# A first product pair taken before the norm's divisor, modulation products moved, and empty scatter slots skipped, in a two-network transformer kernel

## What is computed

```
mod = silu(c) @ ada_w[i] + ada_b[i]             # 1024 -> 6 * 1024: shift, scale, gate, twice
h = modulate(rms_norm(x, norm_g[i, 0]), sh_a, sc_a)      # x/rms * g * (1 + scale) + shift
y = mixer(h)
x = x + g_a * rms_norm(y, norm_g[i, 1])
h = modulate(rms_norm(x, norm_g[i, 2]), sh_f, sc_f)
y = square(relu(h @ ffn_w1[i])) @ ffn_w2[i]              # 1024 -> 4096 -> 1024
x = x + g_f * rms_norm(y, norm_g[i, 3])
```

```
mod = silu(c) @ w_mod[l] + b_mod[l]                      # and the same for a context vector
a = silu(xb @ w_gate[e]) * (xb @ w_up[e]);  yb = a @ w_down[e]
routed = zeros.at[slot_tok].add(yb * slot_w)
```

## Time and profile before

| what | us |
|---|---|
| runs, median (lowest to highest) | 3743.69 (3739.06 to 3747.0), 3 runs |
| the profiled execution: its own time | 3742.4 |
| its span, first to last instruction | 3740.7 |
| PE busy | 3328.8 (89%) |
| DVE busy | 1403.1 (38%) |
| ACT, POOL busy | 504.6 (13%), 427.4 (11%) |
| HBM read and written | 849.95 MB and 36.18 MB, 237 GB/s over the span |

### The profile page before, as it was taken

One profiled execution on the slowest core, in us unless ns is written; L12 is line 12 of the kernel. 1 busy time (PEld: TensorE's weight loads), 2 busy tenths in 40 slices (PEclk: granted clock), 3 DMA queues, 4 the chain that ended last, 5 costly groups with the idle time before them and its releaser, 6 DMA issues.

```text
span 3740.7 us, 40275 instructions
## 1 busy us (share of the span) xinstructions
PE 3328.8 (89%) x14228; PEld 2231.6 (60%) x14228; DVE 1403.1 (38%) x3085; ACT 504.6 (13%) x1021; POOL 427.4 (11%) x482
## 2 busy tenths in 40 slices
PE   3799897998999998899998988899894998999998
PEld 2678785887887886778664533344442676333333
DVE  7555515565023564574373322222213033111112
ACT  1210012000011002100031111111111021111111
POOL 0010103001010001000211211111112002000000
PEclk9899999999999999999999899999996999999999
DMA  7567632774434772465200489999994224999984
GB/s 293 188 234 276 234 136 79 290 282 160 156 123 181 292 269 90 148 257 218 100 31 12 169 287 355 384 376 371 364 373 130 90 79 172 373 397 368 416 362 189
DMA packets 136152, 870.05 MB, mean 233 GB/s; under 512 B 19248, under 2 KB 22448, under 8 KB 38448
## 3 DMA queue, kind: packets, MB, share of 16 engines
q1 hardware_dynamic: 94528, 675.32, 45.8%
q0 software_dynamic: 39984, 190.35, 15.5%
q10 hardware_dynamic: 1472, 2.18, 0.2%
HBM read 849.95 MB, written 36.18 MB: 237 GB/s over the span
## 4 chain that ended last, share of the span: by engine, by line
PE 72%; DMA 13%; DVE 9%; issue 4%; ACT 1%; POOL 0%; SPq 0%; POOLq 0%; DVEq 0%; ACTq 0%
PE ps L709 14%; PE ps L999 12%; PE ps L1239 10%; PE ps L982 9%; PE ps L746 8%; DMA ring<-stream_in 8%; PE ps L1261 6%; PE ps L1277 3%; DMA arena<-mod_stream_in 2%; PE ps L1208 2%; DMA moe_out<-arena,slot_out 2%; PE ps L735 1%; DVE arena L1742 1%; PE ps L1176 1%; DVE YS L1844 1%
## 5 line engine op out<-in xcount | busy, mean ns | idle before, releaser
L1239 PE MATMUL ps<-ring,arena 128*64 128x512 f32 (+2 forms) x2112 | 620.7, 633 | 80.1 <-DMA ring<-stream_in 79.9
L1742 DVE SCALAR_TENSOR_TENSOR arena<-arena,cond 128x512 f32<-128x512 f32 x630 | 447.7, 748 | 73.3 <-DMA arena<-mod_stream_in 63.3
L1239 PEld LDWEIGHTS ps<-ring,arena 128*64 128x64 f32 (+2 forms) x2112 | 224.8, 158 | 416.2 <-issue 414.4
L982 PE MATMUL ps<-H,ring 128*128 128x256 f32 x2048 | 454.6, 383 | 14.3 <-ACT H L1439 14.3
L999 PE MATMUL ps<-arena,ring 128*128 128x256 f32 x2048 | 447.0, 380 | 4.3 <-DVE arena L2004 4.3
L982 PEld LDWEIGHTS ps<-H,ring 128*128 128x128 f32 x2048 | 391.6, 193 | 69.0 <-issue 15.7
L999 PEld LDWEIGHTS ps<-arena,ring 128*128 128x128 f32 x2048 | 389.5, 191 | 57.6 <-issue 5.0
L1261 PE MATMUL ps<-ring,arena 128*64 128x512 f32 (+2 forms) x1056 | 313.6, 609 | 16.9 <-DMA ring<-stream_in 8.3
L1417 ACT ACTIVATE arena<-ps 128x512 f32<-128x512 f32 (+2 forms) x359 | 182.8, 509 | 855.8 <-PE ps L709 343.5
L2210 DVE TENSOR_TENSOR arena<-arena,ps 128x256 f32<-128x256 f32 x83 | 35.0, 422 | 658.0 <-ACT arena L1636 658.0
L746 PE MATMUL ps<-H,ring 128*128 128x256 f32 x1024 | 230.1, 388 | 24.6 <-ACT H L1439 14.3
(11 more groups left out here) (251 smaller groups left out, 3082.5 us busy)
## 6 DMA issues: line engine op xcount, KB each, us to landing
ring<-stream_in SPq DMA_DIRECT2D x618, 1024.0 KB
arena<-mod_stream_in POOLq DMA_DIRECT2D x120, 1024.0 KB, 5.1
arena<-mod_stream_in SPq DMA_DIRECT2D x12, 1024.0 KB, 6.2
YS<-mod_stream_in SPq DMA_DIRECT2D x12, 1024.0 KB, 4.9
moe_out<-zeros POOLq DMA_DIRECT2D x10, 256.0 KB, 3.0
moe_in<-YS POOLq DMA_DIRECT2D x1, 2048.0 KB, 7.6
moe_out<-arena POOLq DMA_DIRECT2D x1, 2048.0 KB, 9.3
YS<-moe_out POOLq DMA_DIRECT2D x1, 2048.0 KB, 19.1
```

Source lines behind the costliest of these rows:

```text
L982: m = mm(out[:, i * T:(i + 1) * T], w[:, c * 256 + i * P:c * 256 + i * P + P], h_lat[c], start=(c == 0), stop=(c == DC - 1))
L1239: m = mm(out[at, :], e_xt[:, k % 2, 4 * part + c, at], w[:, c * TC:(c + 1) * TC], start=(part == c == 0), stop=(part == 1 and c == 3))
L1742: ins = stt(acc, w, x, acc, MUL, ADD)
```

## The change

Seven things, by function:

- `first_pair`: for every s the first half pair and the norm's sums are interleaved on PE, chunk by chunk. Its input is ACT's X * gain (no divisor), with the shift as a 257th column; the second half pair follows. The output's divisor is applied by DVE at the eviction (`first_halves`), and the shift's product is added. H is then overwritten with the divided input as before, and pair 1 waits for it.
- `post_norm`: DVE adds all 8 chunks of the residual, one behind each scaled chunk. POOL adds none. The gains of a layer (`mods`) are worked out before the reciprocal.
- `pre_norm`: ACT takes 8 copies and 6 squares, DVE 2 squares.
- `first_mods`: 4 blocks at the start, not 6. Two of them are PE's products with one column (`by_products`), two are DVE's. All 8 pieces have a buffer of their own, and the rope tables come after DVE's first block; its sines (ACT) come after the first latent products. The constants come in more and smaller DMAs.
- The up products' blocks start one pair later, by a table `UP_WORK`. Layer 0 has 5 blocks in a turn there (10 in all, 2 of them its own mod), layer 3 has 3.
- The down products of layer 3 have three mod2 blocks in a turn, two at k = 0 and one at k = 1.
- `records` and the scatter of the first expert stage: an empty slot's index is out of bounds (`FAR` is 4 * TC), and the DMA leaves it out.

```diff
-UP_PER_PAIR = (2, 2, 2, 2)
+UP_WORK = [[[], [(0, 0)], [(0, 1)], [(1, 0), (1, 1)], [(2, 0), (2, 1)], [(3, 0)], [(3, 1), (4, 0)], [(4, 1)]]]
+UP_WORK += [[[], [(0, 0)], [(0, 1)], [(1, 0)], [(1, 1)], [(2, 0), (2, 1)], [(3, 0)], [(3, 1)]] for _ in range(1, DEPTH - 1)]
+UP_WORK += [[[], [(0, 0)], [(0, 1)], [(1, 0)], [], [(1, 1)], [(2, 0)], [(2, 1)]]]
+def down_jobs(l, k):
+    return ([[0, 1], [2, 3]] if l < DEPTH - 1 else [[0, 1], [2]])[k]
...
+        order["first", 2 * l + 1] = Phase([4], 0)
         mod_banks = [6] if l < DEPTH - 1 else [6, 5]
-        per = UP_PER_PAIR[l]
-        order["ffn_up", l] = Phase([b for j in range(8) for b in [j % 4] + (mod_banks if j % per == per - 1 else [])], 8, 2)
-        order["ffn_down", l] = Phase([b for k in range(2) for b in [k] + mod_banks + ([6, 5] if l < DEPTH - 1 else [])], 8, 2)
+        order["ffn_up", l] = Phase([b for j in range(8) for b in [j % 4] + mod_banks * len(up_done(l, j))], 8, 2)
+        order["ffn_down", l] = Phase([0, 6, 6, 5, 1, 6, 6, 5] if l < DEPTH - 1 else [0, 6, 5, 6, 5, 1, 6, 5], 8, 2)
...
-    stretches = {("start", 0): [("mod", 0)] * 6, ("mla", 0): [("mod", 0)] * 6}
+    stretches = {("start", 0): [("mod", 0)] * 4, ("mla", 0): [("mod", 0)] * 6}
     for l in range(DEPTH):
         nxt = ("mod", l + 1) if l < DEPTH - 1 else ("mod2", 0)
-        stretches["up", l] = [nxt] * (8 // UP_PER_PAIR[l])
-        stretches["down", l] = [nxt, ("mod2", 1)] * 2 if l < DEPTH - 1 else [nxt] * 2
-    piece = step = 0
+        stretches["up", l] = [("mod", l)] * (up_blocks(l) - 4) + [nxt] * 4 if l < DEPTH - 1 else [nxt] * 3
+        stretches["down", l] = [nxt, ("mod2", 1)] * 2 if l < DEPTH - 1 else [nxt] * 3
...
-FAR = 2 * TC
+FAR = 4 * TC
...
+                def by_products(i):
+                    outs = [bank(PLAN["mod", 0], 5 * (i // 2) + 1 + q) for q in range(4)]
+                    for half in range(2):
+                        weights, loaded, n = mod_piece_at(("start", 0), i, half, 0)
+                        pe.wait_ge(loaded, n)
+                        for q in range(4):
+                            for c in range(4):
+                                m = mm(outs[q][0][:, 0:1], weights[:, c, q * P:(q + 1) * P], cond[:, 4 * half + c, 0:1],
+                                       start=(half == c == 0), stop=(half == 1 and c == 3))
+                            if half:
...
+                pe.wait_ge(cond_ready, 2)
+                by_products(1)
+                pe.wait_ge(consts_loaded, 64)
+                mod_columns(PLAN["mod", 0], 0, ("start", 0), 0, 0)
+                by_products(3)
+                mod_columns(PLAN["mod", 0], 5, ("start", 0), 2, 0)
...
+            def first_pair(s, ph):
+                w, used = take(ph, 0)
+                w = w.rearrange("p (c n) -> p c n", c=DC)
+                out, full = bank(ph, 0)
+                out1, full1 = bank(PLAN["first", s], 0)
+                norm, norm_full = bank(PLAN["norm", 2 * s], 0)
+                for c in range(DC):
+                    pe.wait_ge(h_raw, 9 * s + c + 2)
+                    m = mm(out[:, 0:T + 1], w[:, c, 0:P], raw_input(c), start=(c == 0), stop=(c == DC - 1))
+                    if c == 0 and used is not None:
+                        m.then_inc(used, 1)
+                    if c == DC - 1:
+                        m.then_inc(full, 1)
+                    if c < 6:
+                        pe.wait_ge(sq_act, 8 * s + c + 1)
+                    else:
+                        pe.wait_ge(sq_dve, 4 * s + c - 5)
+                    m = mm(norm[:, 0:T], ones_d, SQ[:, c, :], start=(c == 0), stop=(c == DC - 1))
+                m.then_inc(norm_full, 1)
+                for c in range(DC):
+                    m = mm(out1[:, 0:T + 1], w[:, c, P:2 * P], raw_input(c), start=(c == 0), stop=(c == DC - 1))
+                    m.then_inc(h_raw_taken if c < DC - 1 else full1, 1)
...
+                l, shift0 = s // 2, (s % 2) * 3 * DC
+                act.wait_ge(mod_ready, l + 2 if s else 1)
+                fn(H[:, :, T:T + 1], mod[:, l, shift0:shift0 + DC].rearrange("p (c o) -> p c o", o=1), ACT.Copy).then_inc(h_raw, 1)
+                for c in range(DC):
+                    act.wait_ge(*((x_added, 8 * (s - 1) + c + 1) if s else (x_loaded, 16)))
+                    fn(H[:, c, 0:T], X[:, c, 0:T], ACT.Copy, scale=gains[:, l, 2 * (s % 2), c:c + 1]).then_inc(h_raw, 1)
+                    if c < 6:
+                        fn(SQ[:, c, :], X[:, c, 0:T], ACT.Square).then_inc(sq_act, 1)
...
+                for c in (6, 7):
+                    dve.wait_ge(*((x_added, 8 * (s - 1) + c + 1) if s else (x_loaded, 16)))
+                    tt(SQ[:, c, :], X[:, c, 0:T], X[:, c, 0:T], MUL).then_inc(sq_dve, 1)
                 reciprocal_deviation(2 * s)
                 for c in range(DC):
+                    if c < DC - 1:
+                        dve.wait_ge(h_raw_taken, 7 * s + c + 1)
+                    else:
+                        wait_filled(dve, PLAN["first", s], 0)
                     stt(H[:, c, 0:T], X[:, c, 0:T], gains[:, s // 2, 2 * (s % 2), c:c + 1], RSTD[:, 0:T], MUL, MUL)\
                         .then_inc(h_scaled, 1)
+            def first_evicted(s, b, i, out):
+                v.tensor_copy(first_shift[:, i:i + 1], ps[:, b, T:T + 1])
+                link(tt(out, ps[:, b, 0:T], RSTD[:, 0:T], MUL))
+                return ts(out, out, first_shift[:, i:i + 1], None, ADD)
...
-                for c in range(DC):
-                    stt(Y[:, c, :], Y[:, c, :], gains[:, s // 2, 2 * (s % 2) + 1, c:c + 1], RSTD[:, 0:T], MUL, MUL)\
-                        .then_inc(y_scaled, 1)
-                for c in range(4, DC):
-                    dve.wait_ge(y_scaled, 8 * s + c + 1)
-                    tt(X[:, c, 0:T], X[:, c, 0:T], Y[:, c, :], ADD).then_inc(x_added, 1)
+                for c in range(DC + 1):
+                    if c < DC:
+                        stt(Y[:, c, :], Y[:, c, :], gains[:, s // 2, 2 * (s % 2) + 1, c:c + 1], RSTD[:, 0:T], MUL, MUL)\
+                            .then_inc(y_scaled, 1)
+                    if c:
+                        dve.wait_ge(y_scaled, 8 * s + c)
+                        tt(X[:, c - 1, 0:T], X[:, c - 1, 0:T], Y[:, c - 1, :], ADD).then_inc(x_added, 1)
...
-                        stt(slot_out[:, at], token, V("slot", 3), V("slot", 4), ADD, ALU.min)
-                    elif l == 0:
-                        stt(slot_out[:, at], token, float(FAR), V("slot", 1), ADD, ALU.min)
+                        ts(slot_out[:, at], token, V("slot", 3), None, ADD)
...
-                for c in range(4):
-                    pool.wait_ge(y_scaled, 8 * s + c + 1)
-                    g.tensor_tensor(X[:, c, 0:T], X[:, c, 0:T], Y[:, c, :], ADD).then_inc(x_ready, 1)
...
-                        pool.indirect_dma_start(ff, bass.IndirectOffsetOnAxis(slot_out[:, at:at + 1], 0), e_y[:, k % 2, :], None,
-                                                compute_op=ADD).then_inc(scattered, 16)
+                        rows = slot_out if rounds[k].pair else slot_token
+                        pool.indirect_dma_start(ff[0:LANE_B + cols], bass.IndirectOffsetOnAxis(rows[:, at:at + 1], 0), e_y[:, k % 2, :], None,
+                                                bounds_check=LANE_B + cols - 1, oob_is_err=False, compute_op=ADD).then_inc(scattered, 16)
```

273 lines of the change are left out of this document (163 added, 110 removed).

## The result

| | before | after |
|---|---|---|
| median of the runs, us | 3741.38 | 3704.94 |
| range, us | 3736.75 to 3747.0 | 3703.49 to 3707.74 |
| span of the profiled execution | 3740.7 | 3703.7 |

The ratio is 0.9903 (95% interval 0.9886 to 0.992): 36 us faster, where 105 were forecast. The measured 3705 lies above the upper end of the stated range, 3674.

A forecast was written before the change was run, and what follows sets the result against it. PE bounds most of the span, DVE the start and DMA the first expert stage. Terms 52.6 (transitions) - 3.4 (up) - 9.5 (down) + 24.5 (start) + 41 (scatter) = 105.2 us give 3639, range 3612 to 3674.

The forecast's parts named there:

- Transitions: Between sub-blocks, s = 1 to 7, PE waits on a chain of other engines' work; shortening it gains 52.6 us together.
- The sums' end as the bound: In a transition PE's 16 products, not their inputs, set when the norm's sums end: 206.8 us in layer 0.
- the rival of the clock that does not fall: In transitions PE's 16 products take 6.9 us at full clock; 17 us faster over six or seven, 3622; chance 0.12.
- that of PE staying at 1.2 GHz: After each of the 8 first pairs the clock stays low; at 40 us each, 160 us lost, 3799; chance 0.02.
- The start: Kernel start up to the latent stage's second eviction: two blocks on PE and fewer blocks gain 24.5 us (20 to 28).
- I bound 64 loads of weights by 0.06 and 0.25 us each and take 0.12: At the start, PE's one-column products, shown by no row: 0.12 us a load assumed, 8 us for 64 loads.
- Up and down products of layer 3: PE's waits for DVE's modulation blocks in layer 3: up products gain 5.7 us, down products lose 9.5.
- Four of the 8 waits of 1.6 us stay: Layer 3's up products: with 6 blocks for 8, PE's waits for DVE fall to 9.2 us from 12.7.
- the pace of 7.9 us a half: Layer 3's down products, k = 0: DVE's four halves at 7.9 us each end 29.7 us after PE's start.
- asked for 2.4 us into the other half: Layer 3's up products: a piece is requested 2.4 us into the other half, so consecutive halves wait.
- 42 us; ... so I take it nearly whole: First expert stage: 2140 empty slots dropped at 20.8 ns, less 1, give 42 us; 38 taken, with 3 more +41.
- nothing is skipped in effect: Scatter rival, the extreme: each empty slot still costs a transfer, so the time is 3680; chance 0.04.

The follow-up runs named there:

- the runs on four and two: Changed kernel with layer 3's blocks four a turn in up products, two in down: 3702.08 us; same with early piece requests, start order and shared halves: 3664.38 us.

## Why the prediction was wrong

**Transitions: right.** The sums' end as the bound, half pace at first, pair 1 gapless behind the last 8 products: 20.1 and 19.9 us against 20.7. A transition without other work beside it (s = 2, 4, 6) gained 7.4, 7.4 and 6.3 us where 7.4 was counted. Where pair 1 came later, 21.2 us at s = 3 and 5, the lower clock had lasted longer, and the forecast's one value lies between. No run undid them, so this rests on the traces of both kernels alone. Neither the rival of the clock that does not fall nor that of PE staying at 1.2 GHz came true.

**The start: two steps failed, 17 us together.** "I bound 64 loads of weights by 0.06 and 0.25 us each and take 0.12": measured 0.215, near the upper bound, 13.8 us where 8 were taken, twice, on the path. The Trainium skill's 107 ns a load (TensorE: Matmul & The Clock Gate, section LDWEIGHTS) would make it 6.8 us; for these fp32 loads the trace shows twice that, with the clock at its full level. And the sum had no wait for banks: PE's second block stood 7.4 us behind DVE's copies, which DVE did only after two more pieces; with the copies moved ahead of them the block starts 6.0 us sooner and pair 1 4.7.

**Up and down products of layer 3: mis-sized, 18 us.** "Four of the 8 waits of 1.6 us stay" and the pace of 7.9 us a half. The mechanism was right (a piece asked late and 5.1 us under way), the sizes not: the first wait was 6.6 us where 4.4 were counted, behind a piece that was 7.58 us under way (the others in the chain 5.0 to 6.8); halves came every 8.4 us; and each long wait cost twice, by the fallen clock behind it (L758 1.97 instead of 1.04, 29.52 instead of 27.63). Moving blocks between the stages only moved the waits, as the runs on four and two show. Their cause was the request: asking four steps sooner removed 28 us, more than the whole loss. The forecast read "asked for 2.4 us into the other half" as given and not as something that costs.

**The scatter: the step "42 us; ... so I take it nearly whole" failed, 28 us.** That scatters bound the stage was right (35.5 us a period without them), and what a moved row takes of the engines too (5.6 MB less gave back 19 ns of the 16 engines' time a row, 20.8 forecast). Wrong was to turn a mean share over 16 engines into time. The rows gave back 6.4 points of share, 2.6 us a period. Of this the weights took back 0.9 (2.3 points of share for the same bytes), and the rest is idle: a share of 0.97 where it was 1.02. Shown is that the place of dropped rows decides (59 us between two runs that move the same rows; 36.9 us a period when they are dropped evenly), and that the gathers' uneven filling cost 11 us in the kernel before. By the assignment above the fullest engine had 468 rows to move in ten periods and still has 456: in a solo round the low half of the partitions is full before and after. **Still open** is that assignment itself, which is fitted and not tested, why the same weights take more engine time, and what gives the 4 us before the first scatter.

None of the rivals names what happened. The nearest in time was "nothing is skipped in effect", 3680 with a chance of 0.04, but rows are skipped. The shortfalls of the start, of layer 3 and of the scatter, 17, 18 and 28, are 63 of the 69 us.

## What to carry over

A share of DMA time freed on the average is worth nothing until the fullest engine has less: before counting dropped rows as time, ask which partitions they lie in, and compare a run with the rows not issued. Where a request for data has an offset written for one kind of block, check it for the others; a late request can be paid at more than the usual latency (7.58 us here, 5.1 in the median), and again in the clock. A new use of an engine whose cost no row shows belongs near the worse bound when it lies twice on the path.

## What the runs showed of the hardware

- Dropping rows of an accumulating scatter by the bound check: with the 64 rows of the upper half dropped a period is 40.6 us, as in the changed kernel, which drops empty slots alone (40.7); with 64 dropped evenly it is 36.9, nearly as with 64 issued (36.7). A dropped row's own record is 8 bytes and about 10 ns. The page's count of HBM bytes written, 36.18 MB, is the same with rows dropped and not; issued as 64 it is 23.07 MB.
- A scatter of 128 rows lands in 10.3 us with 36% of its rows dropped (5.6 of 15.7 MB), in 8.2 when 64 are issued, in 6.0 when 16 are.
- 32 products of one column (fp32, x64 in the trace, 128x128 loads) take 13.8 us, nearly as long as 32 products of 256 columns do at the full clock (14.05 for x64): 0.43 us a product, with one column or 256.
